# Up projection's input split while the projection before it still runs, weight halves split in two parts at two seams, branches merged one by one, residual reloaded in eight pieces

## What is computed

```python
def reference(x, mem, ...):
    x = x + hybrid_mixer(rmsnorm(x, norm_mix), ...)
    x = x + memory_cross_attention(rmsnorm(x, norm_xa), rmsnorm(mem, norm_mem), ...)
    x = x + conv_glu_ffn(rmsnorm(x, norm_ffn), ffn_up, ffn_conv, ffn_down)
    return x
# hybrid_mixer ends so: three branches, merged by gates, and one projection
merged = gate_a * (y_a @ wb_a) + gate_b * (y_b @ wb_b) + gate_c * (y_c @ wb_c)
return merged @ w_out
# memory_cross_attention ends in:  return o @ wo
def conv_glu_ffn(h, w_up, w_conv, w_down):
    up = causal_dwconv(h @ w_up, w_conv)          # 2 x 5632 features, 3 taps
    g, u = jnp.split(up, 2, axis=-1)
    return (jax.nn.silu(g) * u) @ w_down
```

## Time and profile before

| what | value |
|---|---|
| median of three runs | 2063.06 us (2062.83 to 2063.09) |
| profiled execution, its own time | 2064.64 us |
| its span | 2062.8 us |
| mean granted TensorE clock | 0.997 |
| TensorE (PE) busy | 2030.2 us, 98% |
| VectorE (DVE) busy | 1219.1 us, 59% |
| ScalarE (ACT) busy | 892.3 us, 43% |
| DMA engines | mean 184 GB/s, weight queue 54% of the 16 engines' span |

### The profile page before, as it was taken

How to read it: one execution, slowest core, us unless ns; L and a number is a source line. 1 busy time by engine, 2 the same in 40 slices (tenths; PEclk the granted TensorE clock), 3 DMA queues, 4 the chain that set the end, 5 groups by cost and what they waited for, 6 DMA issues and landing times.

```text
span 2062.8 us, 36597 instructions
## 1 busy us (share of the span) xinstructions
PE 2030.2 (98%) x15772; PEld 1963.9 (95%) x15772; DVE 1219.1 (59%) x1322; ACT 892.3 (43%) x869; POOL 27.6 (1%) x47
## 2 busy tenths in 40 slices
PE   7999999999999999999999999999999999999998
PEld 7999999999999999999999999888888888999998
DVE  5677643544544467576565345677778778744443
ACT  4445333434355433455444334544444444433332
POOL 0000000000000000000000000000000000000000
PEclk9999999999999999999999999999999999999999
DMA  8566434565556856556555355656556556556664
GB/s 262 167 200 194 138 113 155 165 199 169 167 170 217 295 176 220 176 179 190 174 194 163 124 160 175 215 185 203 177 189 199 177 194 195 182 179 201 192 187 127
DMA packets 354751, 378.75 MB, mean 184 GB/s; under 512 B 7887, under 2 KB 350707, under 8 KB 353363
## 3 DMA queue, kind: packets, MB, share of 16 engines
q1 hardware_dynamic: 350659, 353.36, 54.0%
q0 software_dynamic: 3984, 23.74, 3.1%
HBM read 366.06 MB, written 11.02 MB: 183 GB/s over the span
## 4 chain that ended last, share of the span: by engine, by line
PE 94%; DVE 2%; ACT 2%; issue 1%; DMA 0%; POOL 0%; SPq 0%; DVEq 0%; ACTq 0%
PE bank L1793 22%; PE bank L1795 21%; PE bank L1794 21%; PE bank L1827 15%; PE bank L1829 8%; PE bank L2004 1%; DVE w_lo L1029 1%; PE bank L1959 1%; ACT w_hi L479 1%; PE bank L2201 1%; PE bank L2182 1%; ACT x_home L479 0%; PE bank L1864 0%; DMA ident<-in_shape_masks 0%; PE bank L1953 0%
## 5 line engine op out<-in xcount | busy, mean ns | idle before, releaser
L1029 DVE TENSOR_TENSOR w_lo<-raw,w_hi 128x2048 fp32r<-128x2048 f32 (+1 forms) x353 | 765.8, 2170 | 624.3 <-ACT w_hi L479 624.1
L479 ACT ACTIVATE w_hi<-raw 128x2048 fp32r<-128x2048 f32 (+2 forms) x355 | 644.4, 1816 | 1094.2 <-PE bank L1795 819.3
L1793 PE MATMUL bank<-x_home,w_hi 128*128 128x256 f32 x2304 | 648.8, 282 | 5.5 <-DVE w_lo L1029 2.5
L1794 PE MATMUL bank<-x_home,w_hi 128*128 128x256 f32 x2304 | 643.2, 279 | 0.0
L1795 PE MATMUL bank<-x_home,w_lo 128*128 128x256 f32 x2304 | 642.7, 279 | 0.0
L1827 PE MATMUL bank<-x_home,w_hi 128*128 128x512 f32 x1408 | 488.7, 390 | 3.6 <-DVE x_home L1675 2.2
L1793 PEld LDWEIGHTS bank<-x_home,w_hi 128*128 128x128 f32 x2304 | 433.1, 188 | 7.5 <-DVE w_lo L1029 2.3
L1794 PEld LDWEIGHTS bank<-x_home,w_hi 128*128 128x128 f32 x2304 | 433.2, 188 | 0.2
L1795 PEld LDWEIGHTS bank<-x_home,w_lo 128*128 128x128 f32 x2304 | 433.1, 188 | 0.0
L1829 PE MATMUL bank<-x_home,w_lo 128*128 128x256 f32 x1408 | 397.0, 282 | 0.0
L1827 PEld LDWEIGHTS bank<-x_home,w_hi 128*128 128x128 f32 x1408 | 264.2, 188 | 60.0 <-DVE xT L1043 1.7
(11 more groups left out here) (295 smaller groups left out, 2139.2 us busy)
## 6 DMA issues: line engine op xcount, KB each, us to landing
raw<-in_w_in SPq DMA_DIRECT2D x52, 2048.0 KB, 8.5
raw<-in_ffn_up SPq DMA_DIRECT2D x44, 2048.0 KB, 8.0
raw<-in_ffn_down SPq DMA_DIRECT2D x32, 1408.0 KB, 6.4
raw<-in_xa_wkv SPq DMA_DIRECT2D x16, 2048.0 KB, 9.1
raw<-in_w_br SPq DMA_DIRECT2D x8, 2048.0 KB, 8.5
raw<-in_w_out SPq DMA_DIRECT2D x8, 2048.0 KB, 8.2
raw<-in_xa_wq SPq DMA_DIRECT2D x8, 2048.0 KB, 8.1
raw<-in_xa_wo SPq DMA_DIRECT2D x8, 2048.0 KB, 8.1
```

The source lines that it names most:

```text
L479: return nc.scalar.activation(out_, in_, func, **kw)
L1029: tt(split_out(w_lo, kind, half), halves(raw, kind, half, par), split_out(w_hi, kind, half).bitcast(f32), ALU.subtract).then_inc(lo_ready, 1)
L1793: mm(o, w[0], x[0], start=start, stop=False)
L1794: mm(o, w[0], x[1], start=False, stop=False)
```

## The change

Between XO and UP, the first seven tiles of `x_hl` are split while TensorE still does XO's last half: TensorE counts up `x_free` when it has passed two blocks, and `upper_residual(c)` waits for that. `new_residual` is cut in `residual_square` and `residual_gain`. The weights of UP's first two halves, and of WO's second, are split in two parts of eight blocks each (`hi_part`, `lo_part`), and TensorE waits for each part. The two matmuls on the summed squares stand behind UP's second half instead of before it, and UP's halves 2 and 3 (`m + 2`, `m + 3`) are split before `root` and `inverse`. In `merge`, each branch's product waits for its own branch (`br_t`). Between UP and DN, the halves of DN's second unit are split before or between the last products. `x_back` comes in eight pieces, each after two more of DN's halves. Two semaphores for the constant masks become one.

```diff
@@ gpsimd
-            pool.wait_ge(half_used, 2 * last_unit("UP") + 2)
             pool.wait_ge(spill, 32)
-            pool.dma_start(x_back[...], x_spill).then_inc(back, 16)
+            for c in range(D // CW):
+                pool.wait_ge(half_used, first_half("DN") + 2 * c + 3)
+                pool.wait_ge(back, 16 * (c + 1))
+                pool.dma_start(x_back[:, 2 * c:2 * c + 2, :]..., x_spill[:, c * 2 * SEQ:(c + 1) * 2 * SEQ]).then_inc(back, 16)
@@ scalar
+            def hi_part(part, name, i, par, hp, half):
+                if part == 0:
+                    act.wait_ge(raw_full[par], hp * 16 + 16)
+                    act.wait_ge(half_used, hp * 4 + (2 * par + half - 1))
+                ks = slice(part * (KC // 2), (part + 1) * (KC // 2))
+                copy(split_out(w_hi, FM, half)[:, ks, :], halves(raw, FM, half, par)[:, ks, :]).then_inc(hi_ready if part else wp_h, 1)
...
             merged_hi(COUNT["BR"] - 2, 1 - last_unit("BR") % 2)
-            hi_half(*half_of(first_half("WO") + 1))
+            hi_part(0, *half_of(first_half("WO") + 1))
+            hi_part(1, *half_of(first_half("WO") + 1))
             merged_hi(COUNT["BR"] - 1, last_unit("BR") % 2)
...
             def upper_residual(c):
+                if c < 7:
+                    act.wait_ge(x_free, c + 1)
+                else:
+                    act.wait_ge(half_used, first_half("UP"))
                 act.wait_ge(x_g, c + 1)
...
             (p0, h0), (p1, h1) = slot_of("UP", 0), slot_of("UP", 1)
-            hi("UP", 1, p1, h1)
             minor_part(0, 0)
@@ vector
             def merge(i, par, hp):
-                dve.wait_ge(half_used, hp * 4 + (2 * par + 2))
...
+                dve.wait_ge(br_t, i * 2 + 1)
                 tt(m0, bank[par][:, :], gate(0), ALU.mult)
+                dve.wait_ge(br_t, i * 2 + 2)
                 tt(m1, bank[2 + par][:, :], gate(1), ALU.mult).then_inc(br_c, 1)
                 dve.wait_ge(br_c, i * 2 + 1)
                 tt(m0, m0, m1, ALU.add).then_inc(br_c, 1)
                 dve.wait_ge(br_c, i * 2 + 2)
+                dve.wait_ge(half_used, hp * 4 + (2 * par + 2))
                 tt(m1, bank[4 + par][:, :], gate(2), ALU.mult).then_inc(dve_evac, 1)
...
             merge(COUNT["BR"] - 1, u % 2, u // 2)
-            lo_half(*half_of(first_half("WO") + 1))
+            lo_part(0, 2, *half_of(first_half("WO") + 1))
             merged_lo(COUNT["BR"] - 1, u % 2)
+            lo_part(1, 2, *half_of(first_half("WO") + 1))
...
-            dve.wait_ge(back, 32)
             def finish(c, par):
+                dve.wait_ge(back, c * 16 + 32)
@@ tensor
-            project("XO", x_hl, 1)
+            project("XO", x_hl, 1, COUNT["XO"] - 1)
             m = first_half("UP")
-            product_half(m, x_hl, (n_lo, 8, 2))
+            product_half(m - 2, x_hl)
+            product_half(m - 1, x_hl, None, x_free)
+            product_half(m, x_hl, (n_lo, 8, 2), parts=3)
+            product_half(m + 1, x_hl, parts=4)
             pe.wait_ge(x_add, COUNT["XO"])
             ...                                     # the two matmuls on the squares, as before
-            product_half(m + 1, x_hl)
             project("UP", x_hl, 1)
```

More of the change, by code:

```diff
@@ L1030, in lo_half, with lo_part @@
                    split_out(w_hi, kind, half).bitcast(f32), ALU.subtract).then_inc(lo_ready, 1)
+            def lo_part(part, n, name, i, par, hp, half):
+                dve.wait_ge(*((hi_ready, hp * 4 + (2 * par + half + 1)) if part else (wp_h, n)))
+                ks = slice(part * (KC // 2), (part + 1) * (KC // 2))
+                tt(split_out(w_lo, FM, half)[:, ks, :], halves(raw, FM, half, par)[:, ks, :],
+                   split_out(w_hi, FM, half)[:, ks, :].bitcast(f32), ALU.subtract).then_inc(lo_ready if part else wp_l, 1)
             def lo(name, i, par, hp):
@@ L1823, in half_unit @@
                     for k in range(KC if name == "UP" else 0):
+                        if parts and k == KC // 2:
+                            pe.wait_ge(lo_ready, whole)
                         if ready and k % ready[2] == 0:
@@ L1836, in half_unit, with product_half @@
                                      k == cuts[g], k + 1 == cuts[g + 1])
+                        if kind == BR and half and k + 1 in cuts[1:3]:
+                            last.then_inc(br_t, 1)
+                        if passed is not None and k % 2 and k + 1 < KC:
+                            last.then_inc(passed, 1)
                 last.then_inc(half_used, 1)
-            def product_half(m, acts=x_hl, ready=None):
+            def product_half(m, acts=x_hl, ready=None, passed=None, parts=None):
                 name, i, par, hp, half = half_of(m)
@@ L1843, in product_half @@
                     wait_bank(name, i)
-                half_unit(name, i, par, hp, half, acts, ready)
+                half_unit(name, i, par, hp, half, acts, ready, passed, parts)
             def project(name, acts, start=0, stop=None):
@@ L2145, in _ @@
             product_half(m, x_hl, (m_lo, 0, 2))
-            product_half(m + 1, x_hl)
+            product_half(m + 1, x_hl, parts=2)
             project("WO", x_hl, 1, 3)
```

79 lines of the change are left out of this document (46 added, 33 removed).

## The result

The changed kernel took 2052.64 us, median of four (2052.24 to 2053.85), and the kernel before 2063.07 us (2062.83 to 2064.49): 10.4 us less, ratio 0.9947 with a 95% interval of 0.9935 to 0.9958. Two later sets of runs gave 0.9946 (0.9933 to 0.9958) and 0.9945 (0.9932 to 0.9959), with 11.7 and 11.3 us between the medians. Forecast were 12.0 us less, 2051.1, in a range of 2050.2 to 2054.8. The interval of the first ratio is 8.7 to 13.4 us less, so these times alone don't tell 10.4 from 12.0.

The account below looks back on a forecast made before the run. The prediction took TensorE's matmuls (busy 98%) to bound the kernel, with gains only in its idle stretches. The seams' 1.6 + 4.2 + 6.2 = 12.0 us, off the median 2063.06, gave 2051.1 us, range 2050.2 to 2054.8.

Parts of the forecast that it names:

- What bounds it, and the three seams: TensorE, busy 98% of 2062.8 us; gain only in its idle stretches at BR to WO, XO to UP, UP to DN.
- BR to WO, with 0.1 us to spare: TensorE's wait at block 14 of WO's first half goes, `merged_lo` ready 0.1 us early: gain 1.6 us, bounds 1.2 and 1.63.
- XO to UP: Waits at UP's first halves go: 4.26 us less 0.1 lost later, gain 4.2 us, bounds 1.5 and 4.4.
- the late chain behind the square root: UP: root, reciprocal, taps, then weights of half m+4 at E+12.15, wanted at E+12.2; loss 0.1 us, bounds 0 and 0.5.
- UP to DN, clock included: Stall before DN's third half and the clock's fall behind it both go: gain 6.2 us, bounds 3.7 and 6.3.
- 3.68 + 2.6: UP to DN: 3.68 us of stall plus 2.6 us from DN's third half running at the lower clock, together 6.3 us.
- The rival that the clock's part isn't there in timed runs: At UP to DN, timed runs lack the clock's fall: gain 9.4 us, 2053.7 us, chance 0.11.
- The residual in pieces costs nothing: DN's first 62 us: eight `x_back` loads of 256 KB replace 2048 KB; nothing saved, at worst 0.2 us lost for each.
- `w_hi` in DN starts waiting for `raw`: A sign in the changed kernel's profile, in DN, by which the prediction called itself wrong; no size given.
- The margin of 1.85 us: DN's weight loads: 8.25 us from refill of a `raw` slot until it is wanted, for a load that takes 6.4.
- The sum, carried to the median: Whole kernel: 12.0 us gain, worked out on a profiled execution 1.58 us above the median, taken from the median 2063.06: 2051.1 us.
- TensorE's busy time: Whole kernel: busy time falls by some 3 us from 2030, since the slow matmuls are gone.

Follow-up runs that it names:

- whole_halves: The changed kernel with the weight halves of WO (second) and UP (first two) split whole again: 2055.63 us against 2052.87 for the changed kernel.
- filler_matmuls: The kernel before with 16 unused 512-column matmuls ahead of TensorE's wait for DN's third half: ratio 0.9989 to the kernel before.

## Why the prediction was right, and where it was off

- *What bounds it, and the three seams.* Right. The gain lies in TensorE's stalls at these seams: together they make 12.2 of the 12.3 us between the two profiles (the drift and the last 0.5 us nearly cancel), and each gave what its step said within 0.15 us. Part of that closeness is luck, as said under the second and the third.
- *BR to WO, with 0.1 us to spare.* Right: VectorE's last tile for WO starts 813.74 - 812.60 = 1.14 us behind the first weight part, where 1.2 was worked out, and TensorE's steps there are even. `whole_halves` shows that the split in parts carries half of it.
- *XO to UP.* The mechanism is right, the late chain behind the square root included: with E the start of the matmuls on the squares, 1313.00, its last weight split ends at 1322.82 + 2.29 = E + 12.11, where E + 12.15 was worked out. One term was too large and stood in the sum twice: the matmuls on the squares were taken at their modelled 1.02 us and take 0.68 from start to start. So TensorE wanted those weights some 0.3 us sooner, and 0.30 us were lost and not 0.1; and the old stall was some 0.3 us longer than 4.26. The two errors nearly cancel, and the gain of 4.22 us meets the forecast of 4.2 in part by luck.
- *UP to DN, clock included.* The mechanism is right (`filler_matmuls` shows the clock's part by itself), but its size was read from one execution. The term "3.68 + 2.6" is 3.68 + 1.7 in the second profile of before and in the two others with the stall. With 1.7 in its place the sum is 11.1 us; the two later comparisons of medians, 11.7 and 11.3, lie between that and 12.0. That the profiles of before and after are 6.24 us apart at this seam only repeats the execution from which the term was read. The rival that the clock's part isn't there in timed runs was the right doubt in too sharp a form: the part is there, and smaller in three of four profiles.
- *The residual in pieces costs nothing.* Right as to the pieces; their landing took 6.1 us and not the 2.8 of the `out` stores, as each is issued beside a load of weights, and there was room even for twice as many. But the prediction called itself wrong if `w_hi` in DN starts waiting for `raw`, and that came: at 1866 in all three profiles. The sign was drawn too sharply. The margin of 1.85 us was missed at the weights' load beside the last piece and the first store, the one split came 1.0 us late, and TensorE did not wait. What I missed is what the old way would have cost: I worked out only the price of the new loads, and not that, with the stall gone, the one load of 2048 KB would cost TensorE 1.2 us. So the third seam's 6.2 us are the reorder's and the pieces' together: the reorder alone gave 4.4. By medians the parts add up: 1.14, 4.23 and 4.44 us for the seams and 1.9 for the pieces make 11.7, each known to within some 2 us.
- *The sum, carried to the median.* The 1.6 us between forecast and first result are within the noise of the two medians. The changed kernel repeats (2052.64, 2052.90, 2052.87); what moves is the kernel before, 2063.07 in its first four executions and 2064.08 to 2064.60 in the three later groups, which brings the difference from 10.4 to 11.7 and 11.3. The profiled execution of before was 1.58 us above the median of the first three and that of after 0.40 us below its own, so the difference of these two executions, 12.4 us, is at the upper end. The clock explains 0.9 us of the 1.2 us between the two profiles of before. The rest is a slow drift in loops far from the change. It shows in ScalarE's splits of BR's weights, the same code in two kernels; first the changed kernel, then the one with the reload in one piece:

```profile
742.86 1.92 ACT L481 ACTIVATE w_hi<-raw 128x2048 fp32r<-128x2048 f32 x1 [2.91 <-PE bank L1833]
...
754.06 1.92 ACT L481 ACTIVATE w_hi<-raw 128x2048 fp32r<-128x2048 f32 x1 [2.77 <-PE bank L1833]
```

```profile
743.28 1.92 ACT L478 ACTIVATE w_hi<-raw 128x2048 fp32r<-128x2048 f32 x1 [3.02 <-PE bank L1830]
...
754.59 1.92 ACT L478 ACTIVATE w_hi<-raw 128x2048 fp32r<-128x2048 f32 x1 [2.88 <-PE bank L1830]
```

A unit takes 11.20 us in the one and 11.31 in the other, and it goes on so for several units. It is not a wait: TensorE is busy throughout at a granted clock of 1.00 in both, and its mean step is 0.1167 us in the one and 0.1178 in the other. In busy time by stretch, in the same order, the second gets through fewer matmuls:

```profile
700.00:800.00 100.00, 100.00 (x858) 99.89 (x857) 63.85 (x54) 38.80 (x27) 0.00 (x0) 1.00 0.62 199
```

```profile
700.00:800.00 100.00, 100.00 (x851) 99.98 (x850) 64.10 (x54) 38.03 (x27) 0.00 (x0) 1.00 0.62 199
```

It comes and goes from one execution to the next of the same kernel: between 985 and 1010 us the mean step is 0.1178 us in the first profile of before and 0.1166 in the second. What causes it stays open; no run here was made for it.

- *TensorE's busy time.* It was to fall by some 3 us from 2030.2. It fell by 5.5, to 2024.7; from the 2027.9 of the second profile of before it fell by 3.2.

## What to carry to other kernels

When TensorE is at 98%, read the loss of each stall from start to start and add what the clock does behind it, but take the clock's part from several profiles of the same kernel before it goes into a sum (here 2.6 us in one and 1.6 to 1.7 in three). Read a short group of matmuls start to start as well: four of them showed 1.02 us and took 0.68. When a stall goes, look at what it was hiding: a long transfer that cost nothing beside an idle TensorE (here 2048 KB) costs 1.2 us once the engine runs through, and the same bytes in eight pieces cost nothing that can be seen. At a seam where VectorE is the late engine, splitting a weight half in two parts pays: three halves so split, one of them with a tile of activations between its parts, were worth 2.5 to 2.8 us, for about 0.1 us more of ScalarE's and VectorE's time for each.

## What the runs showed of the hardware

- The same stall of 3.52 us of idle time was followed by a granted clock of about half in all four profiles that have it. In three the first matmul behind it was already slow, and the half behind it took 2.6, 1.6 and 1.7 us longer; in one it slowed down only after 1 us at full speed, and took 1.7 us longer.
- Sixteen matmuls of no use in that stall kept the granted clock at 1.00 and made the kernel 2.2 us faster (0.4 to 3.9).
- At a granted clock of 1.00 and without a wait, TensorE's mean step in the same loop was 0.1167 us in some executions and 0.1178 in others. The cause is open.
- Transfers of 256 KB issued beside loads of 1408 KB took 6.1 us to land (median), and the loads 7.1; issued one half, 3.85 us, earlier in the same rhythm they took 3.1, and the loads 6.3.
